# The first modulation as a split product, and the norm made chunk by chunk

## What is computed

```python
m = jax.nn.silu(cond) @ w_mod + b_mod          # cond: one vector for latent, one for context tokens
shift1, scale1, gate1, shift2, scale2, gate2 = jnp.split(m[:, None, :], 6, axis=-1)
h = _rmsnorm(x, norm1_g) * (1 + scale1) + shift1
u = h @ w_in                                   # then attention, pooling and convolution mixers,
                                               # gates, output projection, a gated MLP, a last norm
```

## Time and profile before

| | |
|---|---|
| median of three runs | 1931.54 us |
| the three runs | 1929.78, 1936.9, 1931.54 us |
| span of the profiled execution | 1934.1 us (its device time isn't listed apart from the runs) |
| PE busy, share of the span | 98% |
| VectorE, ScalarE, GpSimd | 61%, 39%, 27% |
| mean granted TensorE clock | 0.994 of full speed |
| first unit matmul | 53.39 us |

### The profile page before, as it was taken

One profiled execution on the slowest core, in us unless ns is written; L12 is line 12 of the kernel. 1 busy time (PEld: TensorE's weight loads), 2 busy tenths in 40 slices (PEclk: granted clock), 3 DMA queues, 4 the chain that ended last, 5 costly groups with the idle time before them and its releaser, 6 DMA issues.

```text
span 1934.1 us, 27395 instructions
## 1 busy us (share of the span) xinstructions
PE 1900.0 (98%) x10412; PEld 1630.0 (84%) x10412; DVE 1176.0 (61%) x2099; ACT 754.1 (39%) x1382; POOL 522.4 (27%) x403
## 2 busy tenths in 40 slices
PE   8899999999999999999999999999999999999999
PEld 3788878888888888878888888888888888888899
DVE  5699895266656765347516855555434444789983
ACT  3512232455555554445322332222222222445464
POOL 0000000544444442124452134444444441000000
PEclk9999999999999999999999999999999999999999
DMA  7471334743343441456551132222222213866664
GB/s 308 162 223 49 112 123 174 169 104 93 92 105 86 104 118 59 158 169 198 161 168 66 58 99 91 86 93 82 71 72 71 71 60 119 301 212 218 215 206 174
DMA packets 226145, 256.32 MB, mean 133 GB/s; under 512 B 37856, under 2 KB 165344, under 8 KB 224992
## 3 DMA queue, kind: packets, MB, share of 16 engines
q1 hardware_dynamic: 226016, 254.58, 42.5%
HBM read 193.98 MB, written 60.56 MB: 132 GB/s over the span
## 4 chain that ended last, share of the span: by engine, by line
PE 87%; DVE 6%; DMA 3%; issue 2%; ACT 2%; SPq 0%; POOL 0%; DVEq 0%; ACTq 0%
PE ps_all L143 62%; PE ps_all L2151 4%; PE ps_all L2152 4%; PE ps_all L2153 4%; PE ps_all L1029 3%; PE ps_all L1052 3%; PE ps_all L1038 2%; PE ps_all L444 1%; DMA branch_and_gates<-branch_dram 1%; DVE X L2639 1%; DVE X L2633 1%; DVE AL L2643 1%; PE ps_all L374 0%; DVE prob L1178 0%; PE ps_all L386 0%
## 5 line engine op out<-in xcount | busy, mean ns | idle before, releaser
L143 PE MATMUL ps_all<-AH,w_hi 128*128 128x512 f32 (+1 forms) x1408 | 507.2, 360 | 8.4 <-DVE wmod_then_mixers L652 3.3
L143 PE MATMUL ps_all<-AL,w_hi 128*128 128x512 f32 (+1 forms) x1408 | 496.2, 352 | 0.0
L143 PE MATMUL ps_all<-AH,w_lo 128*128 128x512 f32 (+1 forms) x1408 | 496.1, 352 | 0.0
L143 PEld LDWEIGHTS ps_all<-AH,w_hi 128*128 128x128 f32 x1408 | 267.7, 190 | 41.7 <-DVE wmod_then_mixers L652 3.5
L143 PEld LDWEIGHTS ps_all<-AH,w_lo 128*128 128x128 f32 x1408 | 267.2, 190 | 36.9
L143 PEld LDWEIGHTS ps_all<-AL,w_hi 128*128 128x128 f32 x1408 | 268.1, 190 | 31.1
L2707 DVE TENSOR_TENSOR quarter<-ps_all,quarter 128x512 f32<-128x512 f32 x140 | 96.5, 689 | 177.3 <-PE ps_all L143 175.3
L2561 POOL TENSOR_TENSOR slot_lo<-w_pair,slot_hi 128x512 fp32r<-128x512 f32 x96 | 130.4, 1383 | 178.9 <-ACT slot_hi L2357 178.9
L1234 POOL TENSOR_TENSOR w_lo<-w_raw,w_hi 128x1024 fp32r<-128x1024 f32 x21 | 50.5, 2404 | 329.4 <-ACT w_hi L1075 329.4
L143 PE MATMUL ps_all<-AH,slot_hi 128*128 128x256 f32 (+1 forms) x384 | 130.3, 339 | 3.4 <-DVE hidden L2678 3.4
L143 PE MATMUL ps_all<-AH,slot_lo 128*128 128x256 f32 (+1 forms) x384 | 129.8, 338 | 0.0
(11 more groups left out here) (263 smaller groups left out, 4102.2 us busy)
## 6 DMA issues: line engine op xcount, KB each, us to landing
w_raw<-w_in_dram SPq DMA_DIRECT2D x42, 512.0 KB
wmod_then_mixers<-w_mod_dram SPq DMA_DIRECT2D x20, 1024.0 KB, 8.3
w_pair<-w_gu_dram SPq DMA_DIRECT2D x20, 1024.0 KB, 5.4
hidden_in<-hidden SPq DMA_DIRECT2D x77, 256.0 KB, 3.2
hidden<-quarter SPq DMA_DIRECT2D x50, 256.0 KB, 2.1
branch_and_gates<-gates SPq DMA_DIRECT2D x16, 768.0 KB, 4.4
w_down_rows<-w_down_dram SPq DMA_DIRECT2D x44, 256.0 KB, 3.7
gates<-gate_rows SPq DMA_DIRECT2D x42, 256.0 KB, 2.3
```

The costliest lines, as they stand in the source:

```text
L143: mm = nc.tensor.matmul(out, w, a[:, k, cols[0]:cols[1]], start=(first and part == 0), stop=(last and part == 2))
```

## The change

Seven things change together.

- **Loads.** All token groups go first, then modulation blocks 0 and 1, unit 0's weights, blocks 2 and 3, and the rest. A block's buffer is free when its low part has been made. The cached keys are loaded ahead of unit 2's weights, and `XT` is spilled right behind these, ahead of the first late modulation block, in place of the time of unit 1.
- **Transposes** go by whole tiles into two pairs of banks; VectorE copies 1024 columns at once. A Sqrt on one element is put ahead of the squares.
- **The product.** The stationary side `c_stack` has 128 columns: two with the high parts of the conditions, two with their low parts, the others zero. Each block of `w_mod` is split into `wm_hi` (ScalarE, two halves) and `wm_lo` (GpSimd for blocks 0, 2 and 4, VectorE for the others), with two buffers. PE multiplies both with `c_stack`. It begins after all transposes and after the spread of `rstd`.
- **Behind it.** The sums are copied out in four pieces, ScalarE and VectorE in turns, turned, and high and low rows are added on VectorE. Unit 1's low part now stands between VectorE's last piece and that addition.
- **The norm** is made by chunk: chunk 0 in pieces of two between the low parts, chunks 1 and 2 one piece after each step of the pair loop. `xn` lies where `AL` will be.
- **The pairs.** The remainders of odd pairs go to GpSimd.
- **Order.** The first six chunks are (0,0), (1,0), (0,1), (0,2), (1,1), (1,2). ScalarE frees the banks of unit 0 within the pair loop, after pairs 11 and 18, and VectorE makes the first GLU piece at step 20 of it.

```diff
-    jobs = [("unit", u, c) for c in range(3) for u in range(2)]
+    jobs = [("unit", u, c) for u, c in ((0, 0), (1, 0), (0, 1), (0, 2), (1, 1), (1, 2))]
...
+        LO_POOL, LO_DVE = (0, 2, 4), (1, 3, 5, 6, 7)
...
-                    sp.wait_ge(w_used, k - 3)
+                    sp.wait_ge(*wmod_lo(k - 4, 1))
...
-                if n >= 2:
-                    load_early(n - 2)
+            for k in range(2):
+                load_early(k)
             load_w(0)
-            for k in range(4, 6):
+            for k in range(2, 6):
                 load_early(k)
             load_w(1)
             for k in range(6, KD):
                 load_early(k)
+            sp.dma_start(cached_k, g.d["cache_k"].rearrange("(t p) n -> p t n", p=P)).then_inc(ck_in, 16)
             load_w(2)
-            sp.dma_start(cached_k, g.d["cache_k"].rearrange("(t p) n -> p t n", p=P)).then_inc(ck_in, 16)
+            sp.wait_ge(xt_ready, NT)
+            sp.dma_start(g.d["xT"].rearrange("k p t -> p k t"), XT).then_inc(spilled, 16)
...
             def early_modulation(k):
-                pe.wait_ge(w_in[k % 4], 16 * (k // 4 + 1))
+
+                if k == 0:
+                    pe.wait_ge(stack_ready, 1)
+                    pe.wait_ge(xt_ready, NT)
                 for q in range(4):
-                    mm = nc.tensor.matmul(rows[:, q * 512:(q + 1) * 512], g.cs[:, 2 * k:2 * k + 2], w_early[:, k % 4, q * 512:(q + 1) * 512],
-                                          start=(k == 0), stop=(k == KD - 1))
-                mm.then_inc(w_used, 1)
+                    out = rows[:, q * 512:(q + 1) * 512]
+                    cols = slice(q * 512, (q + 1) * 512)
+                    if q % 2 == 0:
+                        pe.wait_ge(*wmod_lo(k, q // 2))
+                    nc.tensor.matmul(out, c_stack[:, k, :], wm_hi[:, k % 2, cols], start=(k == 0), stop=False)
+                    mm = nc.tensor.matmul(out, c_stack[:, k, :], wm_lo[:, k % 2, cols], start=False, stop=(k == KD - 1))
+                    if k == KD - 1:
+                        mm.then_inc(row_ready, 1)
+                    elif q == 3:
+                        mm.then_inc(w_used, 1)
...
             pe.wait_ge(silu_ready, 1)
             for n in range(len(X_GROUPS)):
                 turn_rows(n)
-                if n >= 2:
-                    early_modulation(n - 2)
             spread_rstd()
-            for k in range(4, KD):
+            for k in range(KD):
                 early_modulation(k)
             turn_modulation()
-            for c in range(3):
-                for u in range(2):
-                    unit_chunk(u, c)
+            for u, c in ((0, 0), (1, 0), (0, 1), (0, 2), (1, 1), (1, 2)):
+                unit_chunk(u, c)
...
+            def wmod_upper(k):
+                act.wait_ge(w_in[k % 4], 16 * (k // 4 + 1))
+                if k >= 2:
+                    act.wait_ge(w_used, k - 1)
+                for half in range(2):
+                    nc.scalar.activation(wm_hi[:, k % 2, half * D:(half + 1) * D], w_early[:, k % 4, half * D:(half + 1) * D], ACT.Copy).then_inc(wm_split, 1)
...
-            split(0)
-            split(1)
-            act.wait_ge(w_used, KD)
-            nc.scalar.activation(mod_rows[0:2, 0:D], rows[:, 0:D], ACT.Copy).then_inc(rows_out, 1)
+            for k in range(KD):
+                wmod_upper(k)
+                if k == 1:
+                    split(0)
+                elif k == 6:
+                    split(1)
+            for q in (0, 2):
+                act.wait_ge(row_ready, q + 1)
+                nc.scalar.activation(mod_rows[0:4, q * 512:(q + 1) * 512], rows[0:4, q * 512:(q + 1) * 512], ACT.Copy).then_inc(rows_out_act, 1)
             for n in range(len(PAIRS)):
                 upper(n)
+                if n in (11, 18):
+                    evacuate(0, n // 18)
+            evacuate(0, 2)
+            split(2)
...
+            def wmod_lower(k):
+                for half in range(2):
+                    dve.wait_ge(wm_split, 2 * k + half + 1)
+                    if k >= 2:
+                        dve.wait_ge(w_used, k - 1)
+                    cols = slice(half * D, (half + 1) * D)
+                    nc.vector.tensor_tensor(wm_lo[:, k % 2, cols], w_early[:, k % 4, cols], wm_hi[:, k % 2, cols].bitcast(F32), ALU.subtract).then_inc(wm_lowered, 1)
+
+            def normed_rows(c, first, last):
+                a, b = CHUNKS[c]
+                for f in range(first, last):
+                    nc.vector.tensor_tensor(xn[:, f, a:b], XT[:, f, a:b], RB[:, a:b], ALU.mult).then_inc(xn_ready, 1)
...
+            wmod_lower(1)
+            dve.wait_ge(rb_done, 1)
+            dve.wait_ge(xt_ready, NT)
+            normed_rows(0, 0, 2)
             lower(0)
-            dve.wait_ge(rb_done, 1)
-            dve.wait_ge(xt_ready, 2 * NT)
-            for f in range(KD):
-                nc.vector.tensor_tensor(xn[:, f, :], XT[:, f, :], RB, ALU.mult).then_inc(xn_ready, 1)
+            wmod_lower(3)
+            normed_rows(0, 2, 4)
+            wmod_lower(5)
+            normed_rows(0, 4, 6)
+            wmod_lower(6)
+            normed_rows(0, 6, 8)
+            wmod_lower(7)
+            for q in (1, 3):
+                dve.wait_ge(row_ready, q + 1)
+                nc.vector.tensor_copy(mod_rows[0:4, q * 512:(q + 1) * 512], rows[0:4, q * 512:(q + 1) * 512]).then_inc(rows_out_dve, 1)
             lower(1)
-            dve.wait_ge(w_used, KD)
-            nc.vector.tensor_copy(mod_rows[0:2, D:2 * D], rows[:, D:2 * D]).then_inc(rows_out, 1)
             dve.wait_ge(mod_turned, 1)
-            mod_bias(g, 0, 2, mod_cols, mod1)
+            both = mod_cols.rearrange("p (m s j) -> p m s j", s=2, j=2)
+            nc.vector.tensor_tensor(g.mod[:, 0:2 * KD, :], both[:, :, 0, :], g.cols[:, OFF["b_mod"]:OFF["b_mod"] + 2 * KD].rearrange("p (m j) -> p m j", j=1).broadcast_to([P, 2 * KD, 2]),
+                                    ALU.add).then_inc(mod1, 1)
             dve.wait_ge(mod1, 1)
+            nc.vector.tensor_tensor(g.mod[:, 0:2 * KD, :], g.mod[:, 0:2 * KD, :], both[:, :, 1, :], ALU.add).then_inc(mod1, 1)
+            dve.wait_ge(mod1, 2)
             mod_gain(g, 0, "norm1_g", 1, mod1)
-            dve.wait_ge(mod1, 2)
-            dve.wait_ge(xn_ready, KD)
+            dve.wait_ge(mod1, 3)
             for n in range(len(PAIRS) + 1):
                 if n < len(PAIRS) and n % 2 == 0:
                     scaled(n)
-                if n:
+                if n and n % 2:
                     rest(n - 1)
+                if n < 8:
+                    normed_rows(1, n, n + 1)
+                elif n < 16:
+                    normed_rows(2, n - 8, n - 7)
+                if n == 20:
+                    glu_out(0, 0)
             lower(2)
-            glu_out(0)
+            glu_out(0, 1)
+            glu_out(0, 2)
...
+            def rest(n):
+                c, f = PAIRS[n]
+                a, b = CHUNKS[c]
+                pool.wait_ge(ah_ready, n + 1)
+                nc.gpsimd.tensor_tensor(g.AL[:, f, a:b], normed[:, n % 3, 0:b - a], g.AH[:, f, a:b].bitcast(F32), ALU.subtract).then_inc(al_pool, 1)
+
+            nc.gpsimd.memset(c_stack[:, :, :].bitcast(F32), 0.0).then_inc(stack_zeroed, 1)
+            for k in LO_POOL:
+                wmod_lower(k)
+            pool.wait_ge(row_ready, 4)
             nc.gpsimd.memset(ppad, 0.0).then_inc(zeroed, 1)
             for a in (0, HALF + LAT, CB - HALF):
                 last = nc.gpsimd.memset(glu[:, :, a:a + HALF], 0.0)
             last.then_inc(zeroed, 1)
             nc.gpsimd.memset(wp[:, :, :], 0.0).then_inc(zeroed, 1)
+            for n in range(1, len(PAIRS), 2):
+                rest(n)
```

More of the change, by code:

```diff
@@ L227, in token_pieces, with wmod_lo, pair_lo @@
             return [(a, b, 0 if b <= LAT else 1)]
+        def wmod_lo(k, half):
+            if k in LO_POOL:
+                return wm_lowered_pool, 2 * LO_POOL.index(k) + half + 1
+            return wm_lowered, 2 * LO_DVE.index(k) + half + 1
+        def pair_lo(n):
+            return (al_pool if n % 2 else al_ready), n // 2 + 1
         def after(n):
@@ L565, in scalar @@
             nc.scalar.activation(g.cs[:, :], g.cols[:, 0:2 * KD], ACT.Silu).then_inc(silu_ready, 1)
+            act.wait_ge(silu_ready, 1)
+            act.wait_ge(stack_zeroed, 1)
+            nc.scalar.activation(c_stack[:, :, 0:2], g.cs[:, :].rearrange("p (k j) -> p k j", j=2), ACT.Copy).then_inc(stack_hi, 1)
+            act.wait_ge(ones_ready, 1)
+            nc.scalar.activation(tok[:, 1, 0:1], g.eps[:, 0:1], ACT.Sqrt)
             for n, (t0, t1) in enumerate(X_GROUPS):
@@ L643, in modulation, with glu_out @@
                             nc.vector.scalar_tensor_tensor(acc, w, c, acc, ALU.mult, ALU.add).then_inc(acc_step, 1)
-            def glu_out(t):
-                for c in range(3):
-                    n = JOB["unit", 2 * t + 1, c]
-                    dve.wait_ge(done, n + 1)
-                    dve.wait_ge(a_free, 3 * t + c + 1)
```

(25 more changed lines are left out.)

64 lines of the change are left out of this document (34 added, 30 removed).

## The result

The changed kernel takes 1943.0 us (median of 6 runs, 1939.4 to 1943.5); the kernel before, run beside it, 1933.6 (6 runs, 1929.8 to 1936.9). The ratio is 1.0051, interval 1.0040 to 1.0062: slower by 0.5%, 7.7 to 12.0 us. The forecast was 1942.0 and slower by just over 0.5%. The profiled execution took 1943.3, its span is 1941.5.

The account below looks back on a forecast made before the run. TensorE (PE), busy 98% of the span, was taken as the bound. First unit product at 60.8 plus 37.4 gives 98.2 (96.7 with harmless memset), less 87.2: +10.3 taken, 1942 us; range 1933 to 1948.

Parts of the forecast that it names:

- The ruler: End of the sixth first chunk on PE, 87.2 us before; forecast 98.2 or 96.7, taken as +10.3 us.
- Holding, the core of the step: GpSimd subtractions and VectorE's non-PSUM operations take turns; a held one starts when the other ends; product forecast at 54.9.
- the step on which both ends were kept: Ten 128-column diagonals ahead of rstd's spread: if held, sixth chunk ends at 98.2; if not, 94.4.
- Each of the eight blocks 1.8 us ... 14.5 in all: PE's added modulation work: 64 single-pass matmuls at 0.227 us each, replacing 28.3 us of PE.
- rival 3: PE's clock low in the modulation: 3.5 us a block, product at 57.9, sixth chunk 101.3, +14.1, 1945.6 us; chance 0.15.
- the forecast one: Main case, the two engines taking turns: +10.3 us, 1942; chance 0.55, a quarter of it for diagonals not held.
- Memset: GpSimd's 2.29 us clearing after the product: VectorE's subtraction ends at 58.4 if held, 56.9 if not; middle taken.
- The pairs: Six first chunks after the first unit product, limited by late pairs: 37.5 us in sum, 11.5 for chunk (0,0).
- ScalarE's table load: Sign that the forecast is wrong: ScalarE loading a table each time between sigmoid and identity in the pairs.
- The spill: 5 MB store behind unit 2's weights at about 60 us: costs nothing, some 15 us of cover.
- The rest moves with it: PE's work after the sixth chunk shifts by as much as that chunk's end, forecast +10.3 us.

Follow-up runs that it names:

- vector_lo: Changed kernel with all eight low parts of the modulation weights on VectorE, none on GpSimd; median 1935.1 us, ratio 1.0012 to the kernel before.
- beside: Changed kernel with all modulation low parts on VectorE, while GpSimd makes six subtractions whose results nobody uses; ratio 1.0055 to the kernel before.
- spill_back: Changed kernel with the spill of the turned tokens put back at unit 1; median 1944.5 us, ratio 1.0058 to the kernel before.
- order_alone: Kernel before with only the new order of the six first chunks and gate copies inside the pairs; ratio 0.9984.
- gate_first: Kernel before with VectorE's first gated copy moved ahead of its lower part of unit 2; ratio 1.0006.
- gate_and_spill: Kernel before with the first gated copy ahead of unit 2's lower part and the spill issued earlier; median 1928.0 us, ratio 0.9970.

## Why the prediction was nearly right

- **The ruler.** The sixth chunk was forecast at 98.2 (97.5 as taken) and ended at 100.5: +13.3 us where +10.3 was said. The product was 2.5 late against the forecast, the way to the first unit 0.55 short of the middle taken, the pairs 1.1 long. That the time came out 1 us from the forecast is luck: 3 us too little here met 4 us less in the medians than PE's delay.
- **Holding, the core of the step.** Right, and shown by vector_lo and beside. The diagonals, the step on which both ends were kept, are held at 128 columns: 20.8 to 26.9, forecast 21.5 to 27.9. They came early because XT's last copy ended at 20.6, not at 21.4.
- **"Each of the eight blocks 1.8 us ... 14.5 in all".** This term was too small, and with it the product (57.4, forecast 54.9). The held diagonals left PE idle and it worked at 1.2 GHz afterwards: the spread took 4.21 for its last 18 instructions, where all 20 took 2.50 in the kernel before, and the 12 matmuls of block 2's second half and block 3 took 5.5 us where the term gives 2.7. So rival 3 was not another case but partly true inside the forecast one: a hold makes a hole, the hole takes the clock. Its marks, 57.9 and 101.3, lie nearer to the measured 57.4 and 100.5 than the forecast's, though the low clock didn't last through the product (1.00 at 48).
- **Memset.** Forecast with a midpoint; it holds nothing. From the product's end to the first unit product 4.6 us, against 5.9 with a hold and 4.4 without.
- **The pairs.** Forecast 11.5, 5.5, 6.4, 5.8, 5.5, 2.9; measured 11.4, 5.5, 6.4, 6.9, 5.5, 2.9. Only (0,2) was mis-sized, by 1.1. The clock fell to half inside it (matmuls of 256 columns 0.21 apart from 88.9 on in place of 0.12), but that is 0.4 at most: in `beside` and spill_back, at full clock there, it takes 6.5. The other 0.7 is pairs later than forecast. ScalarE's table load (1.28 us at 76.90) came once, not each time. The kernel before has one as well, at 72.56, behind its pairs.
- **The spill** costs nothing and buys nothing in this kernel: right. What was missed is that it is the condition for a gain in the kernel before.
- **"The rest moves with it."** Right to 1104 us. The medians give 9.4 of the 13.3. The profiles' give-back is most likely chance, as above. What stays open: PE's delay against the profile of before (at 102 to 372 us) and the time by the ratio differ in one direction in twelve of the thirteen comparisons, by 0.4 to 4.6 us, in the median by about 2. The medians lie below what PE's delay says. Either the profiled execution of before was quick up to there, or something late in the program takes back a part. Against the first: order_alone, gate_first and gate_and_spill do the same work up to the end of the first chunk and end it at 61.1 to 61.2, before at 61.6. No run here settles it.

## What to carry to other kernels

Before giving GpSimd a share of VectorE's elementwise work, count VectorE's instructions that read SBUF twice or are SBUF-to-SBUF tensor-scalars in that stretch: where they met GpSimd's subtractions here, the two engines took turns, and GpSimd's share went at 2.40 us where VectorE needs 1.2. Ask where the held instruction stands: here ten small ones ahead of PE left it idle and then at half clock. And when a hole is closed, read which load the next engine waits for; the gain was lost to a 5 MB store 20 us further on, and moving that store, which bought nothing in the changed kernel, kept it. (Moved alone in the kernel before, it wasn't run.)

## What was unexpected of the hardware

- A GpSimd memset of 2.29 us left a VectorE subtraction beside it at 1.20; beside GpSimd subtractions that read SBUF the same form took up to 3.36, and in `beside` 2.91 three times in a row.
- Ten tensor-scalars only 128 columns wide took 4.1 us more beside two GpSimd subtractions of 4.66 in all; PE's first two instructions on them, at 23.21, show that one got in between the two.
- The same 1 MB load of the last layer took 5.1 to 8.0 us in fourteen profiles, and PE waited 0.9 to 3.8 us with it.
